# The first norm applied after the transpose, and the modulation's weights taken in items of 1024 columns

## The reference, cut to what matters

```
mod = silu(cvec) @ w_mod[l] + b_mod[l]          # (6, 1024): sh1, sc1, g1, sh2, sc2, g2
h    = rms_norm(x, n1) * (1 + sc1) + sh1
proj = h @ w_in[l]                               # 1792 columns: q, k, v, conv a, conv b
attn = softmax over keys (QK-norm, rotary on the sample); conv = 31 taps, layer norm, silu
x    = x + g1 * (concat(attn, conv) @ w_out[l])
h2   = rms_norm(x, n2) * (1 + sc2) + sh2
x    = x + g2 * moe(h2)                          # 16 experts, 2 per token
```

## Time and profile before

| | us |
|---|---|
| median of 3 runs | 1209.04 (1206.81 to 1209.96) |
| profiled execution | 1206.56 |
| its span | 1204.7 |
| PE busy | 995.3 (83%) |
| VectorE busy | 417.0 (35%) |
| ScalarE busy | 158.1 |
| GpSimd busy | 118.8 |
| DMA | 333.79 MB, mean 277 GB/s |

### The profile page before, as it was taken

The page is one execution under the profiler, slowest core; times in us unless marked ns, Lnnn a source line. Parts: engine busy times, 40 slices in busy tenths (PEclk is TensorE's granted clock), DMA queues, the critical chain, the costliest instruction groups (busy, mean ns, idle before and its releaser), DMA issues.

```text
span 1204.7 us, 11958 instructions
## 1 busy us (share of the span) xinstructions
PE 995.3 (83%) x4410; PEld 465.3 (39%) x4410; DVE 417.0 (35%) x1070; ACT 158.1 (13%) x354; POOL 118.8 (10%) x164
## 2 busy tenths in 40 slices
PE   3799989998879988888819998999688788788891
PEld 2544545556323333333314554555432223323330
DVE  0229879445111111111051987934410111101113
ACT  0110134220000000000021014422000000000001
POOL 0010300511100000000031030051110000000001
PEclk8899979998889999988858997999688889988996
DMA  9984971387899777999985442135666997999825
GB/s 298 390 294 155 229 267 70 101 241 301 349 420 423 304 308 284 427 426 425 402 299 178 140 159 91 35 122 208 256 237 245 424 424 298 399 427 425 341 88 174
DMA packets 78410, 333.79 MB, mean 277 GB/s; under 512 B 6461, under 2 KB 10685, under 8 KB 61925
## 3 DMA queue, kind: packets, MB, share of 16 engines
q1 hardware_dynamic: 56528, 277.89, 58.2%
q0 software_dynamic: 9104, 30.79, 7.2%
q10 hardware_dynamic: 12676, 23.76, 6.8%
HBM read 310.31 MB, written 22.10 MB: 276 GB/s over the span
## 4 chain that ended last, share of the span: by engine, by line
PE 59%; DMA 22%; DVE 11%; SPq 3%; issue 2%; ACT 2%; POOL 1%; ACTq 0%; DVEq 0%; POOLq 0%
PE ps L1568 17%; PE ps L1272 15%; DMA ring<-in_w_up_dram 14%; PE ps L1584 8%; PE ps L1482 7%; DVE scr L943 4%; DMA ring<-in_w_down_dram 4%; PE ps L1294 3%; DMA scr<-h_rows,slot_tok 2%; PE ps L1407 2%; PE ps L1552 2%; DMA ring<-in_w_mod_dram 2%; SPq L364 1%; DMA scr<-expert_rows,pick_y 1%; PE ps L1291 1%
## 5 line engine op out<-in xcount | busy, mean ns | idle before, releaser
L1568 PE MATMUL ps<-ring,hT 128*64 128x512 f32 x1024 | 257.5, 661 | 52.6 <-DMA ring<-in_w_up_dram 40.3
L1568 PEld LDWEIGHTS ps<-ring,hT 128*64 128x64 f32 x1024 | 83.9, 152 | 201.6 <-issue 187.7
L943 DVE SCALAR_TENSOR_TENSOR scr<-scr,convw 128x128 f32<-128x128 f32 (+1 forms) x480 | 160.7, 415 | 0.0
L1584 PE MATMUL ps<-ring,scr 128*64 128x512 f32 x624 | 144.7, 605 | 5.8 <-DVE scr L1235 3.0
L1272 PE MATMUL ps<-ring,hT 128*128 128x512 f32 (+1 forms) x384 | 147.5, 545 | 0.0
L1244 DVE TENSOR_TENSOR scr<-ps,scr 128x256 f32<-128x256 f32 x32 | 13.6, 425 | 351.3 <-ACT scr L831 351.3
L1294 PE MATMUL ps<-ring,cs_rep 128*64 128x256 f32 x640 | 91.5, 447 | 25.9 <-DMA ring<-in_w_mod_dram 25.9
L1272 PEld LDWEIGHTS ps<-ring,hT 128*128 128x128 f32 x384 | 73.4, 192 | 70.7 <-issue 68.4
L1482 PE MATMUL ps<-ring,hT 128*128 128x512 f32 x192 | 84.4, 594 | 1.3 <-ACT hT L698 1.3
L1584 PEld LDWEIGHTS ps<-ring,scr 128*64 128x64 f32 x624 | 48.8, 139 | 89.8 <-issue 85.4
L1294 PEld LDWEIGHTS ps<-ring,cs_rep 128*64 128x64 f32 x640 | 51.6, 161 | 60.7 <-issue 26.6
(11 more groups left out here) (196 smaller groups left out, 770.2 us busy)
## 6 DMA issues: line engine op xcount, KB each, us to landing
ring<-in_w_gate_dram SPq DMA_DIRECT2D x32, 2048.0 KB, 11.5
ring<-in_w_up_dram SPq DMA_DIRECT2D x32, 2048.0 KB, 16.2
ring<-in_w_down_dram SPq DMA_DIRECT2D x32, 2048.0 KB, 20.9
ring<-in_w_mod_dram SPq DMA_DIRECT2D x22, 2048.0 KB, 8.8
ring<-in_w_in_dram SPq DMA_DIRECT2D x6, 2048.0 KB, 19.7
expert_rows<-scr ACTq DMA_DIRECT2D x78, 128.0 KB, 7.6
ring<-in_w_out_dram SPq DMA_DIRECT2D x4, 2048.0 KB, 14.8
expert_rows<-x ACTq DMA_DIRECT2D x1, 6656.0 KB, 36.3
```

Source lines behind the costliest of these rows:

```text
L943: v.scalar_tensor_tensor(out, span, w, out, ALU.mult, ALU.add).then_inc(conv_step[part_], 1)
L1568: mm = pe.matmul(ps[b * TT:(b + 1) * TT, bank, :].rearrange("p (m n) -> p m n", m=2), tokens(k), w[:, :, k, b * HF:(b + 1) * HF], start=(k ...
L1584: mm = pe.matmul(ps[b * TT:(b + 1) * TT, bank, :], src[:, k % 2 * P + k // 2 * TT:k % 2 * P + (k // 2 + 1) * TT], w[:, k, b * SEG:(b + 1) ...
```

## The change

It has five parts.

1. **Items of 1024 columns.** A vector is now two pieces of four k by 1024 columns (`pieces`, 4 KB runs in DRAM in place of 2 KB), `LW` is 512, and `vector(l, j, k0, k1)` on PE replaces `modulation`. `mod_take` takes a whole vector of 512 columns a lane at once, except items 8 and 9.
2. **The first norm in the transposed layout.** DVE makes a diagonal matrix of the reciprocal roots (`scale_tile`), PE multiplies x by it, which transposes and scales in one, and the shift and scale are applied on the way out of PSUM, as per-partition scalars: k 0 to 3 by ACT, k 4 to 7 by DVE (`take_hT`). PE's matmuls of tile 2 wait for tile 0's results.
3. **The scalars come through DRAM.** `columns` stores the two rows and loads them back as columns, 8 numbers (32 bytes) a run. In layer 0 ACT issues it, in layer 1 POOL. The matmuls and copies that spread the vectors at the start are gone, and so are the two 1 MB loads of `mod_a`.
4. **Order of loads and of PE in layer 0.** The four items of `w_in` are loaded right after x, and the gate vector (2) after them. PE computes it behind the projections instead of at the start.
5. **Takes.** Vector 3 (and in layer 0 vector 2) is taken whole ahead of the late taps. PE still computes vector 3 in four pieces, the last after tile 2's transposes. In layer 0's routing the take of layer 1's vector 0 now waits for all of it. POOL's spread of the gate vector moves behind the rotary embedding's roots.

```diff
+def pieces(l, j):
+    if l == LAYERS - 1 and j == 5:
+        return [(VEC[l][j], 0, 4), (LEAD[l] - 1, 4, 6), (LEAD[l], 6, 8)]
+    return [(VEC[l][j], 0, 4), (VEC[l][j] + 1, 4, 8)]
...
+        def columns(eng, l):
+            eng.wait_ge(mod_done, 2 * l + 1)
+            lane_out(eng, mod_dram[:, 0:2 * D], rowA, modA_st[l])
+            eng.wait_ge(modA_st[l], 32)
+            for g_ in range(2):
+                eng.dma_start(modcol[:, g_], mod_dram[g_, 0:2 * D].rearrange("(s p k) -> p s k", s=2, k=KD))\
+                    .then_inc(modcol_in[l], 16)
...
@@ SP @@
             for l in range(LAYERS):
-                for c_ in range(MOD1, MODN):
-                    load_mod(l, c_)
+                if l:
+                    load_vector(l, 2)
                 (the four items of w_in)
-                for c_ in range(MODN, MOD2):
-                    load_mod(l, c_)
+                for j in (2, 3, 4) if l == 0 else (3, 4):
+                    load_vector(l, j)
...
@@ ACT @@
                 if l == 0:
-                    for n in range(4):
-                        act.wait_ge(first_bc_ps, n + 1)
-                        a.copy(scaleB[...], ps[...]).then_inc(first_scale, 1)
-                for t in range(TILES):
-                    take_hT(0, t)
+                    columns(act, 0)
+                act.wait_ge(modcol_in[l], 32)
+                for t in range(TILES):
+                    act.wait_ge(hT_ps, l * 18 + 2 * t + 1)
+                    for m in range(4):
+                        ins = a.activation(hT[:, t, m, :], ps[:, 2 * t % 4, m * P:(m + 1) * P], ACT.Identity,
+                                           bias=modcol[:, group(t), 0, m:m + 1], scale=modcol[:, group(t), 1, m:m + 1])
+                    ins.then_inc(hTa_ready, 1)
...
@@ DVE @@
-            for c_ in range(MOD1 + 1):
-                mod_take(0, c_)
-            (four copies to shiftB)
+            mod_take(0, 0)
...
+                def scale_tile(t):
+                    dve.wait_ge(rstd_ready, l * 6 + t + 1)
+                    v.tensor_scalar(diag[:, t, :], ident, stats(R1 + t), None, ALU.mult).then_inc(diag_ready, 1)
+                def take_hT(t):
+                    dve.wait_ge(modcol_in[l], 32)
+                    dve.wait_ge(hT_ps, l * 18 + 2 * t + 2)
+                    for m in range(4):
+                        k = 4 + m
+                        ins = v.tensor_scalar(hT[:, t, k, :], ps[:, (2 * t + 1) % 4, m * P:(m + 1) * P],
+                                              modcol[:, group(t), 1, k:k + 1], modcol[:, group(t), 0, k:k + 1],
+                                              ALU.mult, ALU.add)
+                    ins.then_inc(hTd_ready, 1)
...
                 if l:
-                    mod_take(l, MOD1)
-                    mod_take(l, MOD1 + 1)
+                    mod_take(l, 2)
                     combine(l - 1, 0)
                     combine(l - 1, 1)
-                norm(0, 0)
-                if l:
+                    scale_tile(0)
                     combine(l - 1, 2)
-                norm(0, 1)
-                norm(0, 2)
+                else:
+                    scale_tile(0)
+                scale_tile(1)
+                scale_tile(2)
                 if l == 0:
-                    mod_take(l, MOD1 + 1)
+                    mod_take(0, 1)
+                for t in range(TILES):
+                    take_hT(t)
...
-                mod_take(l, MODN)
+                if l == 0:
+                    mod_take(l, 2)
+                mod_take(l, 3)
                 for k in range(LATE_TAPS):
                     tap(1, ROPE_TAPS + k)
-                mod_take(l, MODN + 1)
...
@@ PE @@
+                for t in range(TILES):
+                    pe.wait_ge(diag_ready, l * 3 + t + 1)
+                    if t == 2:
+                        hT_first(0)
+                    for n in range(2 * t, 2 * t + 2):
+                        for m in range(4):
+                            mm = pe.matmul(ps[:, n % 4, m * P:(m + 1) * P], x[:, t, 4 * (n % 2) + m::KD], diag[:, t, :],
+                                           start=True, stop=True)
+                        mm.then_inc(hT_ps, 1)
...
                 pe.wait_ge(zT_ready, l * 3 + 3)
-                modulation(l, MODN, 0, KD // 2)
+                if l == 0:
+                    vector(l, 2)
+                vector(l, 3, 0, 2)
                 (per tile t: wait for rope_ready, transposes)
-                    c, k0 = ((MODN, KD // 2), (MODN + 1, 0), (MODN + 1, KD // 2))[t]
-                    modulation(l, c, k0, k0 + KD // 2)
+                    vector(l, 3, 2 * t + 2, 2 * t + 4)
```

More of the change, by code:

```diff
@@ L577, in _ @@
                 if l + 1 < LAYERS:
-                    mod_a(l + 1)
+                    columns(pool, l + 1)
                 for e in range(E):
@@ L1206, in _ @@
                 step.link(v.tensor_tensor(gates[:, :, 1], pmax, wr_, ALU.mult))
-                if l + 1 < LAYERS:
-                    for c_ in range(1, MOD1 - 1):
-                        mod_take(l + 1, c_)
                 dve.wait_ge(pos_ready, l + 1)
@@ L1254, in _ @@
                 if l + 1 < LAYERS:
-                    mod_take(l + 1, MOD1 - 1)
+                    mod_take(l + 1, 1)
                 for e in range(E):
@@ L1317, in _, with vector @@
-            pe.wait_ge(first_scale, 3)
-            modulation(0, MOD1 + 1, 0, KD // 2)
+            def vector(l, j, k0=0, k1=KD):
+                for n, a, b in pieces(l, j):
+                    for k in range(max(a, k0), min(b, k1)):
+                        if n == 0 and k == 0:
+                            pe.wait_ge(first_half, 16)
+                        elif k == (2 if n == 0 else a):
+                            loaded(n)
+                        w = slot_k(slot_of(n), b - a)[:, k - a, :]
+                        for lane in range(LANES):
+                            mm = pe.matmul(ps[lane * LP:(lane + 1) * LP, mod_bank(l, j), :], cs_rep[:, k, :],
+                                           w[:, lane * LW:(lane + 1) * LW], start=(k == 0), stop=(k == KD - 1))
+                        if k == b - 1:
+                            mm.then_inc(slot_used[slot_of(n)], 1)
@@ new lines, in head_fill @@
+            def head_fill(l, hd):
+                c, k0, k1 = HEAD_FILL[hd]
+                if k0 == 0:
+                    pe.wait_ge(mod_taken, taken_at(l, 3 if c == 8 else 8))
+                for n, a, b in pieces(l, 4):
+                    for k in range(max(a, k0), min(b, k1)):
+                        if c == 8 and k == a:
+                            loaded(n)
+                        mm = pe.matmul(ps[0:2, mod_bank(l, c), :], cs_rep[:, k, 0:2],
+                                       slot_k(slot_of(n), b - a)[:, k - a, (c - 8) * SEG:(c - 7) * SEG],
+                                       start=(k == 0), stop=(k == KD - 1))
+                        if c == 8 and k == KD - 1:
+                            mm.then_inc(mod_half_ps, 1)
+                        if c == 9 and k == b - 1:
+                            mm.then_inc(slot_used[slot_of(n)], 1)
@@ L1319, in _ @@
+            vector(0, 0)
+            vector(0, 1)
+            pe.wait_ge(table_in, 16)
             pe.wait_ge(router_in, 32)
@@ L1523, in _ @@
                 router(2)
[L1526 to L1527 removed]
+                vector(l, 5, 0, 6)
                 pe.wait_ge(sel_ready, l + 1)
@@ L1543, in _ @@
                 if l + 1 < LAYERS:
-                    for c_ in range(1, MOD1 - 1):
-                        pe.wait_ge(mod_taken, (l + 1) * MODC - 2 + c_)
-                        modulation(l + 1, c_)
+                    vector(l + 1, 0, 4, KD)
+                    vector(l + 1, 1, 0, 4)
                 pe.wait_ge(pos_ready, l + 1)
```

288 lines of the change are left out of this document (114 added, 174 removed).

## The result

| kernel | median, us | runs | to the kernel before, with 95% interval |
|---|---|---|---|
| before | 1206.81 (1201.93 to 1209.96) | 9 | |
| changed | 1216.74 (1209.98 to 1219.01) | 9 | 1.0074 (1.0049 to 1.0099) |

The forecast was 1208.3, 0.7 faster. The changed kernel is 0.74% slower, some 9 us. Its profiled execution took 1214.43 with a span of 1212.5, 7.8 more than before's 1204.7. TensorE is busy for 990.6, VectorE for 407.9, ScalarE for 158.0, GpSimd for 116.6; DMA moves 331.71 MB.

A forecast was written before the change was run, and what follows sets the result against it. TensorE held 59% of the chain and DMA 22%, with DVE late behind the projections. Terms 4.5 - 6.5 + 2.4 - 0.3 + 5.0 - 4.4 gave 0.7 us faster, 1208.3 from a median of 1209.04; range 1199 to 1217.

The forecast's parts named there:

- Part 1: Layer 0's start: projections stand as if begun warm at 63.1 instead of 67.58, 4.5 us gained, between -5.4 and 10.7.
- The trip: Layer 0's start: storing the columns to DRAM and loading them back takes 12.8 us, between 8.2 and 21.2.
- The 1.5 for longer load runs: Loads ahead of x at the start: longer runs may speed them, 1.5 us taken, from nothing to 3.1.
- 3.4 at most by scaling with columns: Tile 2's eight diagonal matmuls: a quarter of 0.865 us each, 1.73 warm, doubled to 3.4 at half clock.
- the 1.3 for a cold start of the projections: Layer 0's projections: half clock adds 1.3 us beyond the 1.7 on the diagonals.
- Part 2: Behind the projections: DVE stalls at the early takes, delaying late taps and heads; 6.5 us lost in layer 0, 4.4 in layer 1.
- Part 3: Layer 0's experts: without the two 1 MB spreads, expert 3's w_up wait shrinks; 2.4 us gained (0 to 5).
- Part 4: Boundary to layer 1: cheaper norm and diagonal matmuls start its projections sooner; 5.0 us gained, between 3.2 and 6.2.
- the warm branch: Boundary: diagonal matmuls of tiles 0 and 1 raise the clock for layer 1's projections, 6.2 us gained; otherwise 3.2.
- B: Rival at layer 0's start: slow trip, its part becomes -5.4, sum 9.2 us slower, 1218; chance 0.22.
- A: Rival: quick trip, columns landed by 53, and clock up at the boundary; 6.0 us faster, 1203.0; chance 0.34.
- C: Rival behind the projections: takes do not stall, unseen work covers DVE's wait, 10.9 us come back, 1197.4; chance 0.04.

The follow-up runs named there:

- e10: e5 plus eleven 128x512 matmuls into an unused bank in layer 0 while TensorE waits for the columns; 1198.41 us, ratio 0.9923 to the kernel before.
- e2: Changed kernel with the takes of vectors 2 and 3 moved behind the late taps; 1206.02 us, ratio 1.0005 to the kernel before.
- e1: Changed kernel unaltered, run again to see what repeats; 1215.33 us, ratio 1.0084 to the kernel before.
- e3: Kernel before with one line moved: item 7's take ahead of the late taps; 1217.22 us, ratio 1.0094 to the kernel before.
- e5: e2 plus seven f32 128x512 matmuls into an unused bank at layer 1's first gather; 1199.18 us, ratio 0.9928 to the kernel before.
- e6: Kernel before with e5's seven matmuls at layer 1's first gather; 1205.54 us, ratio 0.9988 to the kernel before.
- e11: e2 plus seven one-column matmuls at the place of e5's matmuls; 1201.83 us, ratio 0.9962 to the kernel before.
- e9: e2 plus 14 register moves on TensorE at the place of e5's matmuls; 1205.83 us, ratio 0.9993 to the kernel before.
- e7: e2 plus 64 register moves at the head of TensorE's queue; 1204.51 us, ratio 0.9980 to the kernel before.
- e4: Changed kernel plus 128 register moves at the head of TensorE's queue; 1215.17 us, ratio 1.0081 to the kernel before.
- e8: Changed kernel with take 3 late and layer 0's vector 2 loaded before w_in, multiplied while TensorE awaits the columns; 1208.15 us, ratio 1.0002 to the kernel before.

## Why the prediction was wrong

The order of events that it told was right at nearly every step; the sum was not.

- *Part 1, 4.5 forecast, 2.9 measured.* The trip was right (12.66 for 12.8). The 1.5 for longer load runs was not there: ScalarE's first square starts at 40.63, before at 40.40, though TensorE began on the last `w_mod` piece ahead of x 0.9 sooner (35.50 for 36.39). From the landing to tile 2's matmuls it took 1.6, for 0.9. These matmuls took 4.06, for 3.4 at most by scaling with columns, and e10 shows the scaling wrong at either clock; against that the 1.3 for a cold start of the projections did not come (20.77 for the first 48).
- *Part 2, 6.5 and 4.4 forecast.* The mechanism was right. The segment lengthened by 7.0 in layer 0. In layer 1 the stall is 2.9 (e2), less than 4.4, as the last piece ran at full clock, 1.94 for the 3.23 of the earlier trace rows, and the segment as a whole is only 0.7 longer, since part 4's faster projections lie in it.
- *Part 3, 2.4 forecast.* 2.5 at expert 3, of which 0.6 is left at the last store. What took the rest was not isolated; e1 spreads by 3.4 in that stretch.
- *Part 4, 5.0 forecast.* From the last store to the first projection 39.7 became 37.1, 2.6, and the projections gave 2.2 by the clock: 4.8. That the sum is right is in part luck: the warm branch, priced at 6.2, was taken, and the diagonal matmuls were dearer than priced (11.71 for 48, 3.9 a tile for the 1.7).
- *What failed: the sum's silence on layer 1's experts.* With part 3 the forecast took each stretch that the change doesn't touch to last as before. Layer 1's experts stood in the sum at nothing, and no row was given for it. They became 5.9 longer, with no matmul of an expert edited. The stop ahead of expert 1 came to 2.9 and with it half clock behind it, 3.2 together in the first profile and 5.5 in e1's; the 2.7 that the first profile lost later are a wait for `w_up` and half clock, and nothing was run on them. The 5.9 are over half of the 8.5 between forecast and measured span. The rest is part 1 (1.6), part 3 (about 2) and sizes that partly cancel. What the change did to bring the stop there is open: the experiments show that the stop can be moved, not why it came.
- *The rivals.* B, 1218, has about the measured time by another mechanism, a slow trip, and there was none. A's clock came, its trip did not. C fell: the takes stall, e2 and e3 show it.

Of the two losses one was foreseen and its repair is a matter of order: with the takes late and filler matmuls ahead of layer 1's experts (e5), the change is 0.72% faster than the kernel before, where the same filler alone brings that kernel 0.12% (e6), which is within its noise. The rest of the change, parts 1, 3 and 4 above all, is so worth 5 to 7 us (5.3 between the profiled spans of e6 and e5, 7.2 by the ratios), less than the 11.6 those parts were given.

## What to carry to other kernels

Put a consumer of a late result behind the work that does not need it on an in-order engine: one moved line cost 0.9% (e3, of which the stalls explain about half), and two takes moved the other way gave 0.8% back (e2). When a gain in one stage does not reach the end, compare the untouched stages by milestones before doubting the gain. Where TensorE waits some 10 us ahead of a long run of work, cheap matmuls in the wait are worth a try, though not everywhere: they brought nothing clear in the kernel before (e6) and nothing at the start (e10). A control with equally many matmuls of one column tells clock from placement. A stop that is gone from its place may stand elsewhere: look for it before calling it removed, and see whether it has fallen onto a wait.

## What was not expected of the hardware

- TensorE's stops of 2.1 to 4.3 us with no releaser, 55 in the 14 profiles, all stand in the experts: 38 at the idle matmuls right behind the `If` whose overflow code is not run, 17 at the next group. In each of the 55 a packet of 16 KB on the DMA queue that the profile calls "instruction" starts between 1.2 before the stop begins and 1.7 into it; with 62 to 64 such packets in a profile of some 1200 us, chance would give one stop in four such a packet. In e2 one starts at 880.13, in the stop from 879.82 to 882.78 (DMA queues from 879.8 to 882.8: packets, MB, share):

```profile
q8 instruction: 1, 0.02, 2.4%
```

So the stops go with the loading of the program's own instructions. That TensorE waits for them, and for how much of each stop, no run here shows; many such packets have no stop. Seven one-column matmuls ahead moved a stop of 2.96 on by some 43 us (e11); 14, 64 or 128 register moves did not move it (e9, e7, e4). Of the five stops in the changed kernel's first profile four repeat at the same matmuls in e1; the one at 580.65 does not.

- With the clock at 1.00 an f32 matmul of 128 columns with fresh weights takes 0.51 us (4.08 / 8), and a projection's of 512 columns 0.865: the time did not scale with columns. The Trainium skill's page "TensorE: Matmul & The Clock Gate", "LDWEIGHTS (loading the stationary operand)", has the load's time hang on the stationary operand's columns. The trace agrees as far as it goes: with as many weights and a quarter of the moving columns, well over a quarter of the time was left.
- In e8 the granted clock was at 0.97 in the 2 us from 58 and at 0.50 from 60, with TensorE idle since 57.4; at the boundary it rose under the diagonal matmuls (0.59, then 1.00 from 632), and had not under the transposes with their gaps.
- Runs of 4 KB instead of 2 KB in the `w_mod` loads brought 0.9 at most for the last piece ahead of x (35.50 for 36.39), and nothing for x, which landed at 40.6 for 40.4. The two are not alike, however: the loads of `w_in` were issued from 17.78 on beside x, where before the next load behind x left at 27.39.
